# Stick-breaking attention in spans of 512 keys for both heads, with weights as a sigmoid times a running product

## The chip, the cores and the metric

One core of one Trainium2 chip runs the whole kernel. The metric is device time in microseconds of one launch, the median of three runs. TensorE (PE) multiplies, VectorE (DVE) and ScalarE (ACT) work elementwise and move results out of PSUM, GpSimd (POOL) builds masks and gathers rows, SyncE (SP) issues most transfers. The engines run their own instruction streams in order and meet only at semaphores.

## The reference, cut to what matters

One layer: a projection, three groups of heads side by side (RWKV-7, RG-LRU, stick-breaking attention), an output projection with LayerNorm, then a grouped top-2 MoE with LayerNorm. The change concerns the attention and a little of the MoE. SEQ is 1024, there are 6 attention heads of 64, and queries come in blocks of 128.

```python
def stick_breaking_attention(p, norm_g):
    ...
    for i in range(seq // SBA_BLOCK):
        q0 = i * SBA_BLOCK
        kv_len = q0 + SBA_BLOCK
        z = jnp.einsum('bhtd,bhsd->bhts', q[:, :, q0:kv_len], k[:, :, :kv_len]) * scale
        ...
        mask = s_idx < t_idx
        log_keep = jnp.where(mask, jax.nn.log_sigmoid(-z), 0.0)
        after = lax.cumsum(log_keep, axis=3, reverse=True) - log_keep
        attn = jnp.where(mask, jnp.exp(jax.nn.log_sigmoid(z) + after), 0.0)
        outs.append(jnp.einsum('bhts,bhsd->bhtd', attn, v[:, :, :kv_len]))
    ...
    return head_rms_norm(o, norm_g, SBA_HEADS)
```

So a weight is sigmoid(z) times the product of sigmoid(-z) over all later keys that the mask lets through.

## The kernel before

**Stages.** 0 to 373 us: projection, RG-LRU and the elementwise part of RWKV-7. 373 to 900: the RWKV-7 state recurrence in 12 batches, with the attention woven into it. 900 to 1036: output projection, LayerNorm, router logits. 1036 to 1080: routing. 1080 to 1560: MoE, 21 rounds of two experts. 1560 to 1604: last LayerNorm.

**Batches.** The recurrence is worked off by `mats_pe`, `mats_act` and `mats_dve`, for 3 pairs of heads times 4 batches. A batch starts with products and transposes (L646, L656, L660), masks them on DVE (L765), then inverts a triangular matrix in five levels: PE multiplies (L602, 8 small products), ACT copies the result (L742), PE multiplies twice (L602), DVE keeps parts of the two results (L762, one copy for T under `lower`, one for U under `upper`), and the next level starts once T is there. Then come L683 to L707, and four state steps (L719, L726 on PE, L797 on DVE) with `keep_clock` products on PE in between (L629). Below, a level window is the time from one U copy to the next, the tail is from the last U copy to the next batch, the seam is the start of a batch up to its first U copy.

**Attention units.** `side_by_side` runs such a generator and calls `sba_pe`, `sba_act` or `sba_dve` at each of its 16 gaps, always the next step j. A unit is one head and one query tile with all its keys (128 to 1024), 48 units, 4 steps each. Tiles come in the order 0, 7, 1, 6, 2, 5, 3, 4. Step kinds for unit u: kind 0, PE writes z (L917) and the mask (L919) to PS0, ACT takes |z|, exp and ln (L965, L967, L969); kind 1, DVE takes max(z, 0) (L997); kind 2, DVE scans (L977) and subtracts (L979); next unit's kind 0, ACT takes exp (L951). The weights are then transposed on PE (L932) in kinds 1 and 2, copied by DVE (L989), and multiplied with v (L940) in kind 3; ACT copies the output out (L955). The scan of the unit in a batch's last gap is put off to the batch's end.

**Norms.** After every fourth batch `rnorm_*` normalizes the RWKV heads of the pair and `snorm_*` those of finished attention pairs: sums on PE (L336), Ln and Exp on ACT (L857, L859; L1014, L1016), products on DVE (L872, L874, L877; L1026), with four attention steps in between. The next batch, or the output projection (L1123), waits for them.

**MoE round.** Products of gate and up (L1499), transposes of the next round's rows (`xg_transposes`, L1493), transposes of the hidden rows (L1529, L1534) after DVE's products (L1585), copies (L1589 on DVE, L1564 on ACT), product of down (L1499).

## Time and profile before

| what | us |
| --- | --- |
| three runs | 1601.74, 1605.48, 1607.90 |
| median | 1605.48 |
| profiled execution | 1605.52 |
| its span, first to last instruction | 1603.8 |
| projection and elementwise parts | 373 |
| batches with attention, and the norms among them | 527 |
| output projection, norm, logits | 136 |
| routing | 44 |
| MoE | 480 |
| last norm | 44 |

The profiled execution took 1605.52 us, of which 1603.8 lie between its first and last instruction. PE is busy for 89% of the span, DVE 37%, ACT 27%, POOL 6%; PE's granted clock was 0.944 of full on average. In rows of a timeline the first number is the start, the second the length, both us; the bracket tells how long the engine had been idle and what released it. In rows of groups, "busy, mean ns of one" stands behind the count.

### The profile page before, as it was taken

The page shows a single profiled execution, that of the slowest core. Times are in us where ns is not written, and L with a number is a line of the kernel's source. Part 1 is how long each engine was busy: PE and PEld are TensorE (multiplying, and loading weights), DVE is VectorE, ACT ScalarE, POOL GpSimd, SP SyncE. Part 2 cuts the span into 40 slices and gives each one's busy share as a digit, 9 for nine tenths or more (in the row PEclk, how much of TensorE's full clock was granted, in tenths as well). Part 3 has the DMA queues.
Part 4 walks back from the last instruction along what each step waited for, and adds up shares of the span by engine and source line. Part 5 has one row for each costly group of instructions (what it writes and reads, how often), then busy time and mean ns, then how long its engine had stood idle before and what let it go on. Part 6 is the DMA issues. An engine that isn't in the chain of part 4 may idle for free.

```text
span 1603.8 us, 22792 instructions
## 1 busy us (share of the span) xinstructions
PE 1422.8 (89%) x9346; PEld 763.4 (48%) x9346; DVE 597.4 (37%) x1010; ACT 431.4 (27%) x671; POOL 102.7 (6%) x177
## 2 busy tenths in 40 slices
PE   8999999998888788887888999839999999999980
PEld 3444444455666566655666455514444444444430
DVE  2143103444667566656666333361011101111017
ACT  1044123322444334443434311121111111111113
POOL 0000000001000000000000000000110111111110
PEclk9999999999999988997999999859999999999995
DMA  4110111000000000002000225068749949959415
GB/s 185 38 40 31 35 39 40 27 0 1 1 2 2 1 1 2 1 2 106 1 2 2 81 92 210 27 238 299 271 137 352 338 128 320 340 168 317 117 32 217
DMA packets 61012, 170.14 MB, mean 106 GB/s; under 512 B 3184, under 2 KB 3328, under 8 KB 60928
## 3 DMA queue, kind: packets, MB, share of 16 engines
q1 hardware_dynamic: 54384, 145.31, 24.4%
q0 software_dynamic: 6544, 23.62, 6.1%
q8 instruction: 63, 1.03, 0.3%
q14 instruction: 21, 0.17, 0.0%
HBM read 144.28 MB, written 24.64 MB: 105 GB/s over the span
## 4 chain that ended last, share of the span: by engine, by line
PE 74%; DVE 15%; ACT 4%; issue 4%; DMA 2%; SPq 0%; DVEq 0%; POOL 0%; POOLq 0%; ACTq 0%
PE PS L1499 27%; PE PS L193 16%; PE PS L1123 7%; PE PS L602 4%; PE PS L917 3%; DVE TT L977 3%; PE PS L202 3%; DVE XS L762 2%; PE PS L940 2%; DVE XS L765 2%; PE PS L1493 1%; PE PS L932 1%; PE PS L336 1%; DMA YT<-x1d,RK 1%; PE PS L683 1%
## 5 line engine op out<-in xcount | busy, mean ns | idle before, releaser
L1499 PE MATMUL PS<-RK,YT 128*64 128x512 f32 x736 | 323.6, 596 | 0.8 <-DVE YT L1589 0.8
L193 PE MATMUL PS<-XS 128*128 128x512 f32 x672 | 294.6, 598 | 7.1 <-DMA XS<-in_xT 6.9
L1499 PE MATMUL PS<-XS,YT 128*64 128x512 f32 x656 | 287.3, 595 | 6.4 <-DVE YT L1589 5.5
L193 PEld LDWEIGHTS PS<-XS 128*128 128x128 f32 x672 | 127.3, 191 | 172.6 <-issue 164.2
L1499 PEld LDWEIGHTS PS<-XS,YT 128*64 128x64 f32 x656 | 89.0, 138 | 171.8 <-issue 170.7
L602 PE MATMUL PS<-XS 64*64 64x64 f32 x2688 | 110.9, 231 | 36.3 <-DVE XS L762 24.7
L602 PEld LDWEIGHTS PS<-XS 64*64 64x64 f32 x2688 | 95.1, 143 | 54.6 <-DVE XS L762 39.1
L1585 DVE TENSOR_TENSOR YT<-YT,PS 128x256 f32<-128x256 f32 x42 | 15.8, 419 | 271.8 <-PE PS L1499 271.8
L1123 PE MATMUL PS<-RK,YT 128*128 128x512 f32 x256 | 111.1, 593 | 1.1 <-DVE YT L1026 1.1
L1499 PEld LDWEIGHTS PS<-RK,YT 128*64 128x64 f32 x736 | 99.8, 137 | 20.7 <-issue 20.7
L1499 PE MATMUL PS<-SQ,YT 128*64 128x512 f32 x424 | 104.0, 593 | 1.9 <-DVE YT L1589 1.9
L1123 PEld LDWEIGHTS PS<-RK,YT 128*128 128x128 f32 x256 | 48.1, 190 | 59.8 <-issue 57.9
L762 DVE COPY_PREDICATED XS<-lower,PS 128x512 f32<-128x512 uint8 x60 | 43.5, 726 | 80.6 <-PE PS L602 69.7
L1598 DVE TENSOR_SCALAR YT<-PS,RK 128x512 f32<-128x512 f32 x21 | 15.8, 751 | 142.6 <-PE PS L1499 142.6
L977 DVE TENSOR_TENSOR_SCAN TT<-XS,TT 128x128 f32<-128x128 f32 (+7 forms) x48 | 66.0, 1374 | 1.0 <-ACT XS L969 0.5
L917 PE MATMUL PS<-SQ 64*128 64x512 f32 (+3 forms) x144 | 65.1, 562 | 0.6 <-ACT TT L1014 0.6
L742 ACT COPY XS<-PS 128x512 f32<-128x512 f32 x60 | 35.1, 584 | 109.2 <-PE PS L602 108.3
L1499 PEld LDWEIGHTS PS<-SQ,YT 128*64 128x64 f32 x424 | 38.0, 137 | 49.7 <-issue 49.7
L940 PE MATMUL PS<-XS,SQ 128*64 128x128 f32 x432 | 59.8, 285 | 0.0
L762 DVE COPY_PREDICATED XS<-upper,PS 128x512 f32<-128x512 uint8 x60 | 43.2, 720 | 36.0 <-PE PS L602 35.4
L1488 POOL DMA_INDIRECT sums<-YT,RK x21 | 33.6, 1600 | 328.9 <-DVE YT L1598 328.9
L1499 PE MATMUL PS<-YT 128*64 128x512 f32 x120 | 53.6, 593 | 0.0
(361 smaller groups left out, 1760.7 us busy)
## 6 DMA issues: line engine op xcount, KB each, us to landing
XS<-in_w_in SPq DMA_DIRECT2D x21, 512.0 KB, 3.2
XS<-in_w_gate SPq DMA_DIRECT2D x5, 2048.0 KB, 12.3
XS<-in_w_upx SPq DMA_DIRECT2D x5, 2048.0 KB, 18.0
XS<-in_w_down SPq DMA_DIRECT2D x5, 2048.0 KB, 9.1
RK<-in_w_gate SPq DMA_DIRECT2D x5, 2048.0 KB, 20.2
RK<-in_w_upx SPq DMA_DIRECT2D x5, 2048.0 KB, 22.6
RK<-in_w_down SPq DMA_DIRECT2D x5, 2048.0 KB, 13.1
SQ<-in_w_gate SPq DMA_DIRECT2D x4, 2048.0 KB, 21.3
```

Source lines behind the costliest of these rows:

```text
L193: m = e.matmul(acc[:, half * HB:(half + 1) * HB], XS[:, 8 + n % 4, kt * P:(kt + 1) * P], XS[:, kt, half * HB:(half + 1) * HB], start=kt == ...
L202: m = e.matmul(acc[:, 0:SBA_W], XS[:, kt, i * P:(i + 1) * P], wv[:, kt, :], start=kt == 0, stop=kt == KT - 1)
L602: ins = e.matmul(acc[r, m * P + d * C:m * P + (d + 1) * C], left[r, m, r], right[r, m, r], start=True, stop=True)
L742: e.copy(M1[:, :, :], four(RB(3))).then_inc(s_ma, 1)
L762: return e.copy_predicated(x[:, :, :], mask[:, lv:lv + 1, :].broadcast_to([P, 4, P]), src)
L765: e.tensor_tensor(AM[:, m, :, :], four(RB(m)), mask4[:, :, :], ALU.mult).then_inc(s_md, 1)
L917: ins = e.matmul(PS[0][:, lo:hi], SQ[h, g, i * P:(i + 1) * P], SQ[h, 3 + g, lo:hi], start=True, stop=not last)
L940: ins = e.matmul(PS[1][h, HB + (i % 4) * P:HB + (i % 4 + 1) * P], SV[:, st, g * P + hh * HD:g * P + (hh + 1) * HD], ATb[u % 2][:, st * P:( ...
L977: e.tensor_tensor_scan(R_[:, ::-1], E_[:, ::-1], R_[:, ::-1], 0.0, ALU.add, ALU.add).then_inc(s_bd, 1)
L1123: ins = e.matmul(PS[i % 2][:, half * HB:(half + 1) * HB], YT[:, kt, i * P:(i + 1) * P], WO[kt][:, half * HB:(half + 1) * HB], start=kt == ...
L1488: e.indirect_dma_start(sums, bass.IndirectOffsetOnAxis(put_tok, 0), Yb, None, compute_op=ALU.add)\
L1499: ins = e.matmul(acc[r, :], rows[:, r], third_cols(n, k, at, HB), start=start, stop=stop)
```

## The change

**Attention.** A unit is now both heads of a pair, one query tile, and at most 512 keys. Tiles 4 to 7 have two units, the later keys first; 36 units. PE writes z of head 0 and head 1 to the two halves of PS0 in turn. ACT takes sigmoid(-z) and sigmoid(z) for both heads at once. DVE writes 1 (or the carried product) into the last column, scans each head with a running product from the later keys on, keeps the carry, and multiplies once for both heads. Weights are transposed head by head, copied by DVE head by head, and multiplied with v for both heads in turn, in two parts. A unit has 5 steps, a batch uses 15 gaps. A new z waits only for the sigmoids of the unit ahead, no longer for DVE.

Units per pair, in order, as keys per head (tile): 128 (0), 512, 512 (7), 256 (1), 384, 512 (6), 384 (2), 256, 512 (5), 512 (3), 128, 512 (4).

**MoE.** The transposes of the next rows are cut in two halves, the second behind the transposes of the hidden rows, and 16 instead of 10 `keep_clock` products stand ahead of the first round.

```diff
-        GAPS = 16
+        GAPS, KINDS = 15, 5
         def batch_step(b):
-            return GAPS * b + 4 * (b // NQ) - 1
+            return GAPS * b + 4 * (b // NQ)
...
+        SPANS = []
+        for n in range(NPAIR * NT):
+            i = n % NT // 2 if n % 2 == 0 else NT - 1 - n % NT // 2
+            kv = (i + 1) * P
+            cuts = [(HB, kv), (0, HB)] if kv > HB else [(0, kv)]
+            SPANS += [(n, n // NT, i, lo, hi, lo == cuts[0][0], lo == 0) for lo, hi in cuts]
...
-                wait(e, s_bd, BD * u)
+                wait(e, s_ba, BA * u)
+                wait(e, s_na, z_after_norm[0])
...
+                for hh, h in heads:
+                    ins = e.matmul(Z[:, hh, 0:w], SQ[h, g, i * P:(i + 1) * P], SQ[h, 3 + g, lo:hi],
+                                   start=True, stop=not first)
...
-                    e.activation(E_, E_, ACT.Exp).then_inc(s_ba, 1)
...
-                e.activation(E_, PS[0][:, 0:kv], ACT.Abs).then_inc(s_ba, 1)
-                e.wait_ge(s_ba, BA * u + 1)
-                e.activation(E_, E_, ACT.Exp, scale=-1.0).then_inc(s_ba, 1)
-                e.wait_ge(s_ba, BA * u + 2)
-                e.activation(E_, E_, ACT.Ln, bias=1.0).then_inc(s_ba, 1)
+                e.activation(E2[u % 2][:, :, 0:w], Z[:, :, 0:w], ACT.Sigmoid, scale=-1.0).then_inc(s_ba, 1)
+                wait(e, s_bv, u - 1)
+                e.activation(AT2[u % 2][:, :, 0:w], Z[:, :, 0:w], ACT.Sigmoid).then_inc(s_ba, 1)
...
-            e.tensor_tensor_scan(R_[:, ::-1], E_[:, ::-1], R_[:, ::-1], 0.0, ALU.add, ALU.add).then_inc(s_bd, 1)
+            for hh in range(2):
+                e.tensor_tensor_scan(R[:, hh, 0:w - 1][:, ::-1], keep[:, hh, 1:w][:, ::-1], keep[:, hh, 1:w][:, ::-1],
+                                     1.0 if first else carry[:, hh:hh + 1], ALU.mult, ALU.min).then_inc(s_bd, 1)
             wait(e, s_bd, BD * u + 2)
-            e.tensor_tensor(E_, PS[0][:, 0:kv], R_, ALU.subtract).then_inc(s_bd, 1)
+            if not last:
+                e.tensor_tensor(two(carry[:, :]), R[:, :, 0:1], keep[:, :, 0:1], ALU.mult).then_inc(s_bc, 1)
+                wait(e, s_bc, carried[u + 1])
+            wait(e, s_ba, BA * u + 2)
+            e.tensor_tensor(keep, AT2[u % 2][:, :, 0:w], R, ALU.mult).then_inc(s_bd, 1)
...
-                e.tensor_scalar_max(Rl[:, 0:kv], PS[0][:, 0:kv], 0.0).then_inc(s_bd, 1)
...
-            keep_clock(e, PS[0][:, 0:HB], 10)
+            keep_clock(e, PS[0][:, 0:HB], 16)
...
-                xg_transposes(e)
+                xg_transposes(e, 0)
...
+                xg_transposes(e, 1)
...
+                late = [j for j in range(batch_step(b) + GAPS - 3, batch_step(b) + GAPS) if j % KINDS == 2]
+                side_by_side(mats_dve, lambda e, j: sba_dve(e, j, j not in late), e, b)
```

The new program also differs in what the compiler puts between: loads of ACT's function tables. The first place is ACT in the norms behind the last pair (names: TT holds squares and factors, PS0, PS1 and PS3 the sums). Before:

```order
L850 ACTIVATE TT<-RK 128x1024 [waits rwkv_norm_dve]
L1014 ACTIVATE TT<-PS0,consts 128x1024 [waits head_norm_pe]
L1016 ACTIVATE TT<-TT 128x1024 [waits head_norm_act]
L1014 ACTIVATE TT<-PS1,consts 128x1024 [waits head_norm_pe]
L1016 ACTIVATE TT<-TT 128x1024 [waits head_norm_act]
L857 ACTIVATE TT<-PS3,consts 128x1024 [waits rwkv_norm_act,rwkv_norm_pe]
```

Now:

```order
L852 ACTIVATE TT<-RK 128x1024 [waits rwkv_norm_dve]
L1018 ACT_TABLE_LOAD
L1018 ACTIVATE TT<-PS0,consts 128x1024 [waits head_norm_pe]
L1020 ACT_TABLE_LOAD
L1020 ACTIVATE TT<-TT 128x1024 [waits head_norm_act]
L1018 ACT_TABLE_LOAD
L1018 ACTIVATE TT<-PS1,consts 128x1024 [waits head_norm_pe]
L1020 ACT_TABLE_LOAD
L1020 ACTIVATE TT<-TT 128x1024 [waits head_norm_act]
L859 ACT_TABLE_LOAD [waits rwkv_norm_act]
L859 ACTIVATE TT<-PS3,consts 128x1024 [waits rwkv_norm_pe]
```

Each Ln and each Exp has a load of its own ahead of it, here and in the eight tiles of the LayerNorm behind the output projection; before, one load (L234) ahead of the batches served for all. There are 32 loads more, counted in the two programs' lists.

The second place is DVE between two levels of the second batch of the second pair (lower: the T copy, upper: the U copy; PS1: transposed weights; PS0: z; TT: the running sum or product). Before, between levels 3 and 4, one head of 896 keys:

```order
L762 COPY_PREDICATED XS<-upper,PS2 128x512 [waits delta_pe,inverse_transposed_level]
L989 COPY XS<-PS1 128x128 [waits attn_v_in_psum,attn_transposed]
L997 TENSOR_SCALAR TT<-PS0 128x896 [waits attn_act,attn_dve,z_in_psum]
L989 COPY XS<-PS1 128x128 [waits attn_v_in_psum,attn_transposed]
L977 SCALAR_TENSOR_TENSOR TT<-XS,TT 128x896 [waits attn_dve,attn_act]
L979 TENSOR_TENSOR XS<-PS0,TT 128x896 [waits attn_dve]
L762 COPY_PREDICATED XS<-lower,PS3 128x512 [waits delta_pe,inverse_level]
```

Now, in the same batch between levels 4 and 5, two heads of 512 keys:

```order
L764 COPY_PREDICATED XS<-upper,PS2 128x512 [waits delta_pe,inverse_transposed_level]
L999 COPY XS<-PS1 128x384 [waits attn_v_in_psum,attn_transposed]
L980 COPY TT<-carry 128x2 [waits attn_carry_kept,attn_dve]
L983 SCALAR_TENSOR_TENSOR TT<-XS,carry 128x511 [waits attn_act]
L983 SCALAR_TENSOR_TENSOR TT<-XS,carry 128x511
L990 TENSOR_TENSOR XS<-XS,TT 128x1024 [waits attn_act,attn_dve]
L764 COPY_PREDICATED XS<-upper,PS2 128x512 [waits delta_pe,inverse_transposed_level]
```

The max is gone, one scan has become two, and a block of scans and product stands at other gaps: with 5 steps to a unit it falls on odd and even gaps in turn, where before it always fell on the gap ahead of an even level's copies.

The third place is PE at the end of the up product in the loop of a MoE round (YT: gathered or hidden rows). Before:

```order
L1493 MATMUL PS1<-ident,YT 128x128 x7
L1529 MATMUL PS2<-ident,YT 128x128 [waits hiddenT_copied,hidden_done]
L1534 MATMUL PS2<-ident,YT 128x128 [waits hiddenT_copied_2_act,hidden_done_2]
L1499 MATMUL PS3<-XS,YT 64x512 [waits y_dve,hiddenT_copied,y_act,weight_thirds_loaded2]
```

Now:

```order
L1498 MATMUL PS1<-ident,YT 128x128 x3
L1536 MATMUL PS2<-ident,YT 128x128 [waits hiddenT_copied,hidden_done]
L1541 MATMUL PS2<-ident,YT 128x128 [waits hiddenT_copied_2_act,hidden_done_2]
L1498 MATMUL PS1<-ident,YT 128x128 x4
L1505 MATMUL PS3<-XS,YT 64x512 [waits y_dve,hiddenT_copied,y_act,weight_thirds_loaded2]
```

Four of the eight row transposes have moved from ahead of the hidden transposes to behind them.

## Rows read from the trace of the kernel before

**Rows 1.** Stretches: length, busy PE, PEld, DVE, ACT, POOL, clock, DMA share, GB/s.
```profile
373.00:408.20 35.20, 29.23 (x431) 21.16 (x430) 21.17 (x38) 15.65 (x31) 4.64 (x8) 0.95 0.01 2
...
408.20:449.20 41.00, 34.78 (x480) 26.27 (x476) 26.48 (x47) 16.31 (x32) 4.08 (x4) 0.96 0.01 2
...
725.20:771.80 46.60, 40.88 (x471) 29.94 (x471) 26.49 (x43) 17.16 (x32) 2.35 (x4) 0.78 0.24 91
...
sum 527.40, PE 445.41 PEld 323.49 DVE 328.26 ACT 214.32 POOL 31.31; mean PE 29.69 PEld 21.57 DVE 21.88 ACT 14.29 POOL 2.09
```
**Rows 2.** Timeline of PE, first batch, levels with almost no attention.
```profile
381.25 0.68 PE L602 MATMUL PS<-XS 64*64 64x64 f32 x16 [0.42 <-DVE XS L762]
...
384.27 0.68 PE L602 MATMUL PS<-XS 64*64 64x64 f32 x16 [0.42 <-DVE XS L762]
```
**Rows 3.** Timeline of DVE, first batch of the second pair, levels 3 and 4.
```profile
559.49 0.73 DVE L762 COPY_PREDICATED XS<-lower,PS 128x512 f32<-128x512 uint8 x1 [2.93 <-PE PS L602]
...
560.93 1.21 DVE L997 TENSOR_SCALAR TT<-PS 128x1024 f32<-128x1024 f32 x1
562.25 2.29 DVE L977 TENSOR_TENSOR_SCAN TT<-XS,TT 128x1024 f32<-128x1024 f32 x1
564.57 1.23 DVE L979 TENSOR_TENSOR XS<-PS,TT 128x1024 f32<-128x1024 f32 x1
565.71 0.71 DVE L762 COPY_PREDICATED XS<-lower,PS 128x512 f32<-128x512 uint8 x1
```
**Rows 4.** Groups by shape, 373 to 900 us.
```profile
L940 PE MATMUL PS<-XS,SQ 128*64 128x128 f32 x432 | 59.8, 285 | 0.0
...
L917 PE MATMUL PS<-SQ 64*128 64x512 f32 x72 | 43.4, 700 | 0.0
...
L989 DVE COPY XS<-PS 128x512 f32<-128x512 f32 x18 | 12.4, 689 | 6.4 <-PE PS L932 6.4
...
L977 DVE TENSOR_TENSOR_SCAN TT<-XS,TT 128x512 f32<-128x512 f32 x6 | 7.4, 1234 | 0.0
```
**Rows 5.** Timeline of PE, first products of a batch; z of one head, 896 columns.
```profile
372.97 2.10 PE L646 MATMUL PS<-RK 64*128 64x256 f32 x16
...
443.55 1.77 PE L917 MATMUL PS<-SQ 64*128 64x512 f32 x4
```
**Rows 6.** Timeline of DVE at a seam, first pair.
```profile
449.65 2.02 DVE L977 TENSOR_TENSOR_SCAN TT<-XS,TT 128x896 f32<-128x896 f32 x1
```
**Rows 7.** Timeline of ACT, a table load in the projection.
```profile
98.66 1.28 ACT L234 ACT_TABLE_LOAD   x1
99.95 1.15 ACT L320 ACTIVATE RK<-RK,vec 128x1024 f32<-128x1024 f32 x1
```
**Rows 8.** Timeline of ACT, norms behind the last pair.
```profile
895.84 1.06 ACT L1016 ACTIVATE TT<-TT 128x1024 f32<-128x1024 f32 x1
```
**Rows 9.** Timeline of PE and DVE, end of a MoE round's up product.
```profile
1277.12 1.09 PE L1493 MATMUL PS<-ident,YT 128*128 128x128 f32 x8
1277.23 0.76 DVE L1585 TENSOR_TENSOR YT<-YT,PS 128x256 f32<-128x256 f32 x2 [12.81 <-PE PS L1499]
...
1278.05 0.38 PE L1529 MATMUL PS<-ident,YT 128*128 128x128 f32 x2
...
1278.47 0.42 DVE L1589 COPY YT<-PS 128x256 f32<-128x256 f32 x1 [0.49 <-PE PS L1529]
...
1279.04 0.61 PE L1499 MATMUL PS<-XS,YT 128*64 128x512 f32 x1 [0.39 <-DVE YT L1589]
```
**Rows 10.** Timeline of PE ahead of the first MoE round.
```profile
1072.56 4.26 PE L629 MATMUL PS<-restart,identb 128*128 128x512 bf16 x10
...
1077.99 1.09 PE L1493 MATMUL PS<-ident,YT 128*128 128x128 f32 x8 [1.17 <-DMA YT<-x1d,RK]
```
**Rows 11.** A stretch of two microseconds, columns as in rows 1.
```profile
567.00:569.00 2.00, 2.00 (x14) 1.24 (x11) 0.03 (x1) 1.35 (x2) 0.00 (x0) 0.50 0.01 4
```
**Rows 12.** The page's costliest groups, all of the run's U copies behind level products.
```profile
L762 DVE COPY_PREDICATED XS<-upper,PS 128x512 f32<-128x512 uint8 x60 | 43.2, 720 | 36.0 <-PE PS L602 35.4
```

More of the change, by code:

```diff
@@ L907, in sba_pe @@
                     return
-                g, i, hh, h, kv, ng = unit(u)
+                n, g, i, lo, hi, first, last = SPANS[u]
                 wait(e, s_pe, LRU_T + SBA_T + NT)
-                wait(e, s_bd, BD * u)
-                for pair in range(1, NPAIR - 1):
-                    if j == norm_step(pair) + 1:
-                        wait(e, s_na, 2 * (pair - 1) + 1)
-                for lo in range(0, kv, HB):
-                    hi = min(kv, lo + HB)
-                    last = hi == kv
-                    ins = e.matmul(PS[0][:, lo:hi], SQ[h, g, i * P:(i + 1) * P], SQ[h, 3 + g, lo:hi],
-                                   start=True, stop=not last)
-                ins = e.matmul(PS[0][:, kv - P:kv], identb[:, :], causal_neg[:, :], start=False, stop=True)
+                wait(e, s_ba, BA * u)
+                wait(e, s_na, z_after_norm[0])
+                z_issued[0] = u + 1
+                w = hi - lo
+                for hh, h in heads:
+                    ins = e.matmul(Z[:, hh, 0:w], SQ[h, g, i * P:(i + 1) * P], SQ[h, 3 + g, lo:hi],
+                                   start=True, stop=not first)
+                if first:
+                    for hh, h in heads:
+                        ins = e.matmul(Z[:, hh, w - P:w], identb[:, :], causal_neg[:, :], start=False, stop=True)
                 ins.then_inc(s_bz, 1)
@@ L924, in sba_pe @@
                 return
-            g, i, hh, h, kv, ng = unit(u)
-            if kind <= ng:
-                k = kind - 1
-                wait(e, s_ba, BA * u + 4)
-                wait(e, s_bt, groups(u) + k)
-                lo, hi = group(i, k)
-                for st in range(lo, hi):
-                    ins = e.transpose(PS[1][:, (st - lo) * P:(st - lo + 1) * P], Eb[u % 2][:, st * P:(st + 1) * P],
-                                      ident[:, :])
+            n, g, i, lo, hi, first, last = SPANS[u]
@@ L934, in sba_pe @@
+            tiles = range(lo // P, hi // P)
+            if kind <= 2:
+                hh = kind - 1
+                wait(e, s_bd, BD * (u + 1))
+                wait(e, s_bt, 2 * u + hh)
+                for k in range(len(tiles)):
+                    ins = e.transpose(PS[1][:, k * P:(k + 1) * P], E2[u % 2][:, hh, k * P:(k + 1) * P], ident[:, :])
                 ins.then_inc(s_bx, 1)
+                return
+            cut = (len(tiles) + 1) // 2
             if kind == 3:
-                wait(e, s_bt, groups(u + 1))
@@ L937, in sba_pe @@
-                if hh == 0:
-                    wait(e, s_bo, u // 2)
-                for st in range(i + 1):
+                wait(e, s_bt, 2 * u + 2)
+                if first:
+                    wait(e, s_bo, n)
+            ins = None
+            for k in (range(cut) if kind == 3 else range(cut, len(tiles))):
+                for hh, h in heads:
                     ins = e.matmul(PS[1][h, HB + (i % 4) * P:HB + (i % 4 + 1) * P],
-                                   SV[:, st, g * P + hh * HD:g * P + (hh + 1) * HD],
-                                   ATb[u % 2][:, st * P:(st + 1) * P], start=st == 0, stop=st == i)
+                                   SV[:, tiles[k], g * P + hh * HD:g * P + (hh + 1) * HD],
+                                   AT2[u % 2][:, hh, k * P:(k + 1) * P], start=first and k == 0,
+                                   stop=last and k == len(tiles) - 1)
@@ L958, in sba_act @@
                     return
[L959 to L960 removed]
+                w = SPANS[u][4] - SPANS[u][3]
                 wait(e, s_bz, u + 1)
@@ L1503, in moe_pe @@
             ahead(e, s_xgp, s_htp, s_htp2, s_y1)
-            keep_clock(e, PS[0][:, 0:HB], 10)
+            keep_clock(e, PS[0][:, 0:HB], 16)
             e.wait_ge(s_xg, 16)
-            xg_transposes(e)
+            for half in range(2):
+                xg_transposes(e, half)
             e.wait_ge(s_tab, 1)
```

89 lines of the change are left out of this document (42 added, 47 removed).

## The prediction

> **What bounds the kernel now.** I read the stretches first, then the timeline of each engine inside a batch, then the groups by shape. The change sits almost wholly in the 527.4 us of batches and norms; PE is busy 445 of them, DVE 328, ACT 214 [rows 1]. PE's share looks like the bound, but in a batch the engines take turns. A level with next to no attention takes 3.03 us from one first product to the next (381.25 to 384.27), PE, ACT, PE and DVE one after another [rows 2]. Where a block of attention stands on DVE between two levels, the T copy waits for it: with a head of 1024 keys max, scan and subtraction take 1.21, 2.29 and 1.23 us, and 6.22 us pass from T copy to T copy (559.49 to 565.71) [rows 3]. Over all windows I find a length of 3.03 us or of DVE's attention work plus 1.35 us, whichever is more; 4.7 + 1.35 is close to the 6.2 shown. Only where z or v products stand alone does PE set a window. So a batch is a chain that passes through three engines, and takes 35.2 us with little attention and 41.0 with a full share [rows 1].
>
> **PE's attention work.** z takes 43.4 us for the 512-column pieces alone, v products 59.8 [rows 4]. Products on two halves of the rows overlap when they alternate: the 16 instructions of L646 are 8 products of 256 columns, 2048 in all, and take 2.10 us; at the rate of a z, 896 columns in 1.77, they would take 4.0 [rows 5]. With both heads in turn z and v are halved; with the narrower z pieces this is some 64 us of PE's busy time. Transposes stay.
>
> **DVE's work.** The max goes, 1.21 us for 1024 columns. The scan keeps its price for a column: two of 512 are 2 x 1.234 = 2.47 against 2.29 [rows 3, 4]. The product should cost what the subtraction does, 1.23 (the other end, should PSUM have been its limit, is half of that; nearest row taken). A block for 2 x 512 columns is then 2.47 + 1.23 + 0.1 to 0.2 for the ends = 3.8 to 3.9 us, against 4.73 for one head of 1024. Copies keep their shapes mostly, 0.69 for 512 [rows 4]. Summed over 36 units against 48: about 149 against 181 us, 32 less.
>
> **What of it lies on the chain.** I went through the 12 batches gap by gap with these prices; the 60 windows between the U copies [rows 12] now add up to 260 us, the 12 tails to 141 (the norms left out), the 12 seams to 86.
> - Windows. Before, a block falls on the windows ahead of level 2's and level 4's copies, a third into the tail, a fourth is put off. Now two of a batch's three blocks fall into windows and the third is put off, so windows hold more of DVE than before, 55 us above their cover of 1.65 (3.03 less the two copies) against 40. Against it, PE and ACT hold windows up less: 22 us by my count, against 41 now in which slow-clock stretches are included. Of the 22, some 13 are new: when z falls on an even gap, the two sigmoids (2 x 1.06 us [rows 8], 1024 columns) stand ahead of ACT's next level copy and that window grows by some 2 us, z's own time included. Sum of the windows: 255, so -5.
> - Tails. No block stands there any more, and z and v are short: about 10.3 us each against 11.8, -18.
> - Seams. The put-off block runs ahead of the masks, as a scan of 2.02 us and its subtraction do now [rows 6]. In the first pair it is as long as now. In the later pairs it is 1.4 to 3.8 us, where now it is mostly 128 to 384 columns: +8. The first big unit of the third pair now falls behind the norms' last product, ahead of the next masks: +3. Sum +11.
> Together -12 us. It can be anything from -50 (PE sets every window, 64 us and a bit of ACT's relief come through) to +15 (second rival).
>
> **Norms.** Sigmoid, Ln and Exp now each need a table load. One takes 1.28 us, and the next instruction starts 0.01 us behind its end [rows 7]. There are 32 more, 41 us of ACT. Most hide: ACT waits for DVE or PE between norm tiles, and a load that has no wait of its own runs while the engine would be idle. Those on the path: behind the first pair the Exp (1.3, and 1.4 for the block now put off to that place); behind the second pair five loads less the wait for sums that covers one and a half of them, and larger sigmoids, +5; behind the last pair four in the row Ln, Exp, Ln, Exp that the output projection waits for [rows 8], +5.1; at the last LayerNorm tile one, +1.3. Sum +14, between +8 (loads hide behind sums) and +18.
>
> The Trainium skill, "ScalarE: Activation LUTs", section "What ACT_TABLE_LOAD costs", gives 2.66 us for a switch, 1.28 of load and 1.38 of drain. The row shows the first and nothing of the second. With the page's figure the ten or so loads on the path would cost, by estimate, 14 us more.
>
> **MoE.** Between the up product and the down product lie 1.92 us (1277.12 to 1279.04) for eight, two and two transposes, products on DVE and a copy. The hidden transposes start at 1278.05 though the first DVE half is there about 1277.65 (0.42 of the 0.76); the copy starts 0.42 us behind their start and ends at 1278.89, and PE follows 0.15 later [rows 9]. With four row transposes less ahead they start at about 1277.75, the copy ends at 1278.6, PE could go on at 1278.75, and its remaining transposes end there too. 0.29 x 21 rounds = -6 us; bounds 0 and -9. The next gather is issued behind POOL's scatter anyway, far later than the half of a transposition block by which it is now released later. Six more keep_clock products at 0.43 us [rows 10] reach 1079.4 where the rows arrive at 1077.99, against a first product that starts fast: 0, within 1.5 either way.
>
> **Sum.** 1605.5 - 12 + 14 - 6 = 1601.5, against the profiled execution, 1605.52; the median is 1605.48. I take **1601 us**.
>
> **Rivals.**
> - PE is what counts. Its share is highest, and its waits inside a full batch add up to only 6 of 41 us. If DVE's blocks merely fill time that PE's long z and v products (43.4 and 59.8 [rows 4]) would take anyway, two thirds of the 64 us come through: -40 + 14 - 6 = 1574. Against it: the window of rows 3, in which PE waits for DVE.
> - The slow clock. Behind DVE blocks of 3.9 us and more PE stood idle for 2 us or so, and was granted 0.50, that is 1.2 instead of 2.4 GHz, for several us after (567 to 569 [rows 11], right behind the block of rows 3); such a batch took 46.6 us at a clock of 0.78 [rows 1]. With PE's work halved and 23 big blocks in windows and seams against 14, more stretches run slow: nine more at 1 to 2 us, and the same cost as now for the others, which my windows left out, is +22: 1605.5 + 10 + 14 - 6 = 1624. It decides if most full batches run at clocks like that 0.78 and not like the 0.95 and 0.96 of the first two. This is the case on the other side.
> - A table switch costs the load twice, since the engine also has to run empty: ten loads on the path at another 1.28 make +13, 1614. Rows 7 speak against it, the following instruction starting at once; but there both neighbours were long ones. The skill's page named above has such a drain.
> - The change doesn't do what it says: z of two heads doesn't overlap. Then PE's saving is only v's, and the sum moves by a few us, inside the range.
>
> **Chances.** The sum's case 0.40, with its own range 1590 to 1613: 0.10 of it faster, 0.28 the same, 0.02 slower. PE's case 0.33, all faster. The slow clock 0.22, table switches 0.05, both slower. A measurement here can tell about 0.5% from no change, 8 us. So faster 0.43, same 0.28, slower 0.29. The range takes in most of both outer cases: 1564 to 1627.
>
> **What would show it.** Right: T copies wait up to 6 us behind blocks of two scans; three blocks in a batch; tails of about 10 us; ACT loads of 1.28 us, four in the last norms, where the output projection starts some 15 us after the last batch instead of 10; MoE rounds of 22.4 instead of 22.67 us. PE's case: full batches of 37 us. The slow clock: granted clock under 0.85 in full batches, and these over 42 us. Wrong altogether: a product on DVE far cheaper than the subtraction, scans dearer by the column, or z of two heads taking 1.7 us for 2 x 512 columns.

## The result, and the profile after

The changed kernel takes 1625.33 us (median of 4 runs, 1624.39 to 1626.59) against 1605.99 for the kernel before: ratio 1.0131, 95% interval 1.0109 to 1.0153. It is slower by 19 us, where 1601 was forecast. With each later group of runs the kernel before was run again and took 1604.92 to 1606.07 us (medians), so times of different groups can be set side by side to about 1 us. The profiled execution has a span of 1622.7 us against 1603.8, so the two traces show the same 19 us.

I cut both traces along the same instructions: a batch's seam (first product to the first U copy), its windows (U copy to U copy), its tail (last U copy to the next batch), and the norms.

| part, us | before | after | difference | forecast |
|---|---|---|---|---|
| 12 seams | 85.1 | 94.8 | +9.7 | +11 |
| 60 windows | 260.5 | 263.2 | +2.7 | -5 |
| 12 tails | 141.4 | 134.3 | -7.1 | -18 |
| norms between pairs | 30.4 | 40.1 | +9.7 | +7.7 |
| last norms, to the output projection | 10.0 | 15.4 | +5.4 | +5.1 |
| output projection and LayerNorm | 136.5 | 141.0 | +4.5 | +1.3 |
| MoE rounds | 471.1 | 465.3 | -5.8 | -6 |
| sum | | | +19.1 | -4 |

The page of the changed kernel, its first line and the row of PE (in the kernel before PE is busy 1422.8 us):

```profile
span 1622.7 us, 22622 instructions
...
PE 1394.9 (86%) x9352; PEld 708.1 (44%) x9352; DVE 569.8 (35%) x1004; ACT 405.4 (25%) x583; POOL 99.7 (6%) x177
```

PE has 28 us less to do, DVE 28 and ACT 26 less, and still the end comes later. Stretches of the changed kernel (columns as in rows 1), two full batches and the whole attention stage:

```profile
409.60:451.25 41.65, 34.64 (x473) 24.93 (x471) 23.42 (x45) 10.72 (x22) 2.35 (x4) 0.84 0.01 2
...
594.80:638.00 43.20, 34.55 (x475) 24.55 (x471) 23.59 (x45) 11.10 (x22) 2.35 (x4) 0.84 0.01 1
...
372.94:920.71 547.77, 413.70 (x5690) 295.80 (x5689) 298.71 (x543) 163.36 (x297) 28.18 (x48) 0.88 0.03 9
```

The second batch had a clock of 0.96 before and took 41.0 us [rows 1]; now it has 0.84 and takes 41.7. Over the stage the mean granted clock fell from 0.92 to 0.88. Where does PE wait? Groups by shape over 372 to 905 us, first of the kernel before (level products, then the products behind the last level):

```profile
L602 PE MATMUL PS<-XS 64*64 64x64 f32 x2688 | 110.9, 231 | 36.3 <-DVE XS L762 24.7 <-ACT XS L742 10.6
...
L683 PE MATMUL PS<-XS 64*64 64x128 f32 x192 | 17.6, 339 | 3.3 <-DVE XS L762 3.2
```

and of the changed kernel, with z (L916), v (L944) and the U copies:

```profile
L604 PE MATMUL PS<-XS 64*64 64x64 f32 x2688 | 116.4, 238 | 52.1 <-DVE XS L764 29.4 <-ACT XS L744 22.0
...
L764 DVE COPY_PREDICATED XS<-upper,PS 128x512 f32<-128x512 uint8 x60 | 43.0, 717 | 9.5 <-PE PS L604 8.5
...
L944 PE MATMUL PS<-XS,SQ 128*64 128x128 f32 x432 | 40.3, 300 | 3.4 <-DVE XS L999 3.2
...
L916 PE MATMUL PS<-SQ 64*128 64x512 f32 x72 | 27.3, 844 | 2.7 <-ACT TT L1018 2.7
...
L685 PE MATMUL PS<-XS 64*64 64x128 f32 x192 | 19.2, 361 | 18.5 <-DVE XS L764 18.5
```

z and v did shrink (43.4 and 59.8 us in rows 4, now 27.3 and 40.3). In their place PE waits: for DVE 47.9 us at these two lines against 27.9, for ACT 22.0 against 10.6. DVE waits 9.5 us ahead of the U copies, where it waited 36.0 [rows 12]: DVE is now seldom early. And the level products, the same work, take 116.4 us instead of 110.9; with PE's waits filled (experiment 1) they take 106.3 in the changed kernel, so this is the low clock.

One window shows all of it: the changed kernel, sixth batch, PE and DVE.

```profile
606.10 1.15 PE L604 MATMUL PS<-XS 64*64 64x64 f32 x32
606.44 0.95 DVE L983 TENSOR_TENSOR_SCAN TT<-XS 128x383 f32<-128x383 f32 x1
...
607.31 0.93 DVE L983 TENSOR_TENSOR_SCAN TT<-XS 128x383 f32<-128x383 f32 x1
...
608.47 0.96 DVE L990 TENSOR_TENSOR XS<-XS,TT 128x768 f32<-128x768 f32 x1
609.34 0.72 DVE L764 COPY_PREDICATED XS<-lower,PS 128x512 f32<-128x512 uint8 x1
609.95 0.71 DVE L764 COPY_PREDICATED XS<-upper,PS 128x512 f32<-128x512 uint8 x1
...
610.12 0.69 PE L604 MATMUL PS<-XS 64*64 64x64 f32 x16 [2.50 <-DVE XS L764]
...
611.57 1.97 PE L604 MATMUL PS<-XS 64*64 64x64 f32 x32
```

Two scans, carry and product hold the T copy up until 609.34; PE stands for 2.50 us, and soon after its next 32 products take 1.97 us instead of the 1.15 of the first line. The clock of the same place:

```profile
610.00:611.00 1.00, 0.89 (x19) 0.81 (x20) 0.66 (x2) 0.16 (x1) 0.00 (x0) 0.83 0.00 0
611.00:612.00 1.00, 0.85 (x12) 0.48 (x12) 0.00 (x0) 0.70 (x2) 0.00 (x0) 0.50 0.00 0
...
616.00:617.00 1.00, 1.00 (x14) 0.88 (x11) 0.00 (x0) 1.00 (x2) 0.00 (x0) 0.50 0.00 0
```

0.50 is 1.2 instead of 2.4 GHz. By the shares of these rows it begins about 0.5 us after PE took up work at 610.12, and it lasts 6.8 us, through a z and half of the next window.

### The profile page after: what moved, and what is told of

Same layout as the page of the kernel before. It is cut to its first block, busy times and chain, and to the rows that moved or that the text cites. A ratio compares the mean times of both kernels' runs of the same rounds, so it can differ in the third digit from the quotient of the medians.

```text
span 1622.7 us, 22622 instructions
## 1 busy us (share of the span) xinstructions
PE 1394.9 (86%) x9352; PEld 708.1 (44%) x9352; DVE 569.8 (35%) x1004; ACT 405.4 (25%) x583; POOL 99.7 (6%) x177
## 4 chain that ended last, share of the span: by engine, by line
PE 72%; DVE 13%; ACT 6%; issue 5%; DMA 2%; SPq 0%; DVEq 0%; POOL 0%; POOLq 0%; ACTq 0%
PE PS L1505 26%; PE PS L195 16%; PE PS L1128 7%; PE PS L604 4%; DVE TT L983 3%; PE PS L204 3%; PE PS L916 2%; DVE XS L764 2%; DVE XS L767 2%; PE PS L1498 1%; PE PS L933 1%; PE PS L631 1%; DMA YT<-x1d,RK 1%; PE PS L338 1%; PE PS L685 1%
## 5 line engine op out<-in xcount | busy, mean ns | idle before, releaser
L604 PE MATMUL PS<-XS 64*64 64x64 f32 x2688 | 116.4, 238 | 52.1 <-DVE XS L764 29.4
L604 PEld LDWEIGHTS PS<-XS 64*64 64x64 f32 x2688 | 100.5, 150 | 80.0 <-DVE XS L764 42.3
L999 DVE COPY XS<-PS 128x512 f32<-128x512 f32 (+3 forms) x72 | 39.8, 552 | 59.9 <-PE PS L933 59.9
L1505 PEld LDWEIGHTS PS<-SQ,YT 128*64 128x64 f32 x424 | 32.6, 137 | 52.8 <-issue 52.8
L1493 POOL DMA_INDIRECT sums<-YT,RK x21 | 33.6, 1601 | 321.3 <-DVE YT L1606 321.3
L1578 ACT ACTIVATE YT<-PS,RK 128x512 f32<-128x512 f32 x21 | 14.4, 687 | 138.2 <-PE PS L1505 138.2
L226 DVE SCALAR_TENSOR_TENSOR RK<-PS,vec,RK 128x1023 f32<-128x1023 f32 x11 | 14.1, 1283 | 97.6 <-ACT RK L215 97.6
L617 POOL TENSOR_TENSOR XS<-RK,pc 128x256 f32<-128x256 f32 x24 | 14.2, 613 | 548.2 <-PE PS L204 368.2
```

The source lines that it names most:

```text
L604: ins = e.matmul(acc[r, m * P + d * C:m * P + (d + 1) * C], left[r, m, r], right[r, m, r], start=True, stop=True)
L999: e.tensor_copy(AT2[v % 2][:, hh, 0:w], PS[1][:, 0:w]).then_inc(s_bt, 1)
L1493: e.indirect_dma_start(sums, bass.IndirectOffsetOnAxis(put_tok, 0), Yb, None, compute_op=ALU.add)\
L1505: ins = e.matmul(acc[r, :], rows[:, r], third_cols(n, k, at, HB), start=start, stop=stop)
```

## The experiments

Theory: DVE's block of attention is one piece of 3.9 us where a window covers 1.65; PE's narrower work turns into waiting for it, and the longer waits bring the low clock. On top, the table loads cost more than forecast. Rivals: the blocks hold the windows but the clock hits only hidden work; PE's busy time counts for nothing, or for everything; the price of the table loads is not their own length.

**1. Filling PE's waits, in the changed kernel and in the kernel before.** `fill_before` is true where a scan stands in the window, FILL is 6.

```
+                if fill_before(b, lv):
+                    keep_clock(e, RB(3), FILL)
                 wait(e, s_tl, b * NTL + lv)
                 diag_products(e, RB(3), AM[:, :, 1, :], T_, ms)
```

> The changed kernel with six 512-column products that nobody reads put on PE ahead of each level product whose T copy has a DVE block of attention in front of it (some 20 places; at full clock six take 1.3 us, and PE stands idle for 2 to 2.7 us there). Slow-clock theory (the rival with 1624 of the prediction: behind such a wait PE is granted 0.50 for several us, and the stage's mean clock fell from 0.92 to 0.88): the clock of the attention stage rises to 0.93 or more and the time falls by 8 to 18 us, to 1607 to 1617. Rival, the DVE blocks alone hold the windows and the low clock hits only products that are hidden: the clock rises, the time stays within 3 us of 1625. Should the filling itself come late in some windows, up to +5.

1613.33 us, ratio to the kernel before 1.0058 (1.0038 to 1.0077), 12 us less than the changed kernel. The stage's clock up to 850 us is 0.92 instead of 0.88, windows 254.0 us, tails 132.1, seams and norms as they were. The place shown above, with the filling:

```profile
602.61 1.47 PE L631 MATMUL PS<-restart,identb 128*128 128x512 bf16 x6
...
605.18 0.68 PE L604 MATMUL PS<-XS 64*64 64x64 f32 x16 [1.10 <-DVE XS L772]
...
606.63 1.15 PE L604 MATMUL PS<-XS 64*64 64x64 f32 x32 [0.41 <-ACT XS L752]
```

DVE's block is as long as before, only the products behind it are fast again. So these low stretches were on the path. The same in the kernel before, with its own scans:

> The kernel before with the same filling: six 512-column products on PE, read by nobody, ahead of each level product whose window has a DVE scan in it. The prediction took the cost of the slow clock to be the same before and after and left it out of both; the filling took 12 us off the changed kernel. If the low clock is a cost that the change brought: here within 4 us of 1605 (0 gain), or slower, since PE has 22 to 28 us more of z and v work to delay. If both kernels lose alike by it: 8 to 12 us faster, and the low clock doesn't explain the difference between them.

1602.36 us, ratio 0.9983 (0.9968 to 0.9998): 3 us, with the clock at 0.97 instead of 0.91. That is 9 us less than in the changed kernel, but it doesn't follow that those 9 are a cost of the change, for the filling also delays PE where it has work. Two batches of the kernel before with filling, the second and the ninth:

```profile
411.81:454.61 42.80, 37.19 (x491) 27.17 (x488) 26.45 (x46) 16.41 (x32) 4.08 (x4) 0.96 0.01 2
728.82:770.86 42.04, 37.68 (x484) 27.04 (x484) 26.23 (x44) 17.04 (x32) 2.36 (x4) 0.94 0.27 101
```

Without it [rows 1] they took 41.0 us at a clock of 0.96 and 46.6 at 0.78: the first has lost by the filling, the second gained. Window by window, the 14 windows of the kernel before whose clock had been under 0.95 became 12 us shorter and the other 46 became 12 us longer; in the changed kernel 24 such windows became 13 us shorter and the other 36 4 us longer. So low clock in the windows costs both kernels about the same, 12 and 13 us, and most of the 9 us are what the filling itself costs. Each total is a lower bound of what the low clock costs, and the difference of two lower bounds is no bound of anything.

More of the changed kernel does run slow: at half clock are 60 us of its windows against 46 before, 22 of its seams against 14, and 27 of the nine tails with no norm behind against 16. Work at half the clock loses at most half of its length, so these 34 us more can by estimate cost up to 17. How much they do cost no run here shows: the filling doesn't stand in seams and tails.

**2. The DVE block taken apart.** Both scans and the carry stay in `sba_scan`, the product is now `sba_product` and follows two gaps later:

```
             if kind == 2 and scan:
                 sba_scan(e, u)
+            if kind == 4 and scan:
+                sba_product(e, u)
```

> The changed kernel with each DVE block taken apart: both scans and the carry stay where the block was, the product follows two gaps later. Theory that DVE's block holds the chain: a window has some 1.65 us of DVE cover, a block of 2 x 512 columns is 3.9 us, so it costs about 2.2 us of a window; in two pieces of 2.6 and 1.25 us it costs about 1.0. With some 20 such blocks in windows the time falls by 15 to 25 us, to 1600 to 1610, and PE's waits of 2.5 us shrink to 1.3, with fewer stretches at 0.50. Rival, PE and ACT hold the windows (sigmoids on even gaps, v products): within 4 us of 1625, or slower, since transposes of the unit now wait for the later product.

1577.89 us, ratio 0.9826 (0.9797 to 0.9855): 47 us less than the changed kernel, twice what was expected. In the profiled execution, which took 1581.88 us, windows are 233.1 (-30), seams 87.7 (-7), tails 127.5 (-7). 33 of the 60 windows had a clock of 0.95 or more in both traces; they are 13.5 us shorter in all, up to 1.3 us each where a block stood. The other 27, slow in one trace or in both, gave 16.6. The same window as above:

```profile
595.21 0.72 DVE L764 COPY_PREDICATED XS<-lower,PS 128x512 f32<-128x512 uint8 x1
...
595.99 0.68 PE L604 MATMUL PS<-XS 64*64 64x64 f32 x16 [1.52 <-DVE XS L764]
596.44 0.95 DVE L996 TENSOR_TENSOR XS<-XS,TT 128x768 f32<-128x768 f32 x1
...
597.45 1.15 PE L604 MATMUL PS<-XS 64*64 64x64 f32 x32 [0.41 <-ACT XS L744]
```

The product now runs while PE works, PE waits 1.52 us and stays fast. Is the clock's share in the 47? Filling on top of it:

> The changed kernel with scans and product two gaps apart and the same filling. Taking the block apart brought 47 us where 15 to 25 were expected from the cover of a window alone. If the rest came through the clock (shorter waits of PE, fewer stretches at half clock), the 12 us of the filling are in it already: within 3 us of 1578, or slower. If the two are independent: 1566.

1581.29 us, ratio 0.9831 (0.9806 to 0.9855): no gain. The 12 us of the filling and the 47 of the split are not independent. Between the two kernels with filling the split is still worth 32 us (1613.33 against 1581.29), and seams, windows and tails (norms left out) hold 39 instead of 61 us at half clock. Those 22 us can by estimate account for 11 at most, so at least some 20 of the 47 us are the chain itself.

**3. The same treatment for the kernel before**, its subtraction (`sba_minus`) one gap behind its scan:

```
             if kind == 2 and scan:
                 sba_scan(e, u)
+            if kind == 3 and j not in [norm_step(g) for g in range(NPAIR)]:
+                sba_minus(e, u)
```

> The kernel before with its own DVE block taken apart in the same way: the scan stays at its gap, the subtraction follows one gap later (at once in the one unit behind which the head norms run). This asks what the changed form of the weights is worth when both kernels have short pieces on DVE. Theory that the length of one piece of DVE work between two level copies is what costs: a head of 1024 keys leaves pieces of 1.21, 2.29 and 1.23 us, so the time falls by 10 to 25 us, to 1580 to 1595, and the form of the weights itself is worth little. Rival, splitting helps the changed form only, since here the z of the next unit must wait for the subtraction and the pieces of one unit stand in three windows anyway: 1598 to 1615.

1592.57 us, ratio 0.9902 (0.9868 to 0.9935): 13 us; seams 78.6 instead of 85.1, windows 256.5 instead of 260.5. Long pieces on DVE are a cost of both kernels; by these two edits, which are alike but not the same, it is three to four times dearer in the changed one. With both taken apart the changed kernel is 15 us ahead, of which 6 are MoE's.

**4. Table loads.** The three norms' loads by hand; `exp_ln` loads one set that has both functions, `sigmoid_set` that of Sigmoid:

```
+            if snorms(g):
+                exp_ln(e)
             for xg in snorms(g):
                 snorm_act(e, xg, 1)
+            if snorms(g):
+                sigmoid_set(e)
...
+            exp_ln(e)
             wait(e, s_fp, 3 * g + 3)
```

> The changed kernel with the table loads of the head norms placed by hand: one load of the set that holds both Ln and Exp ahead of each Ln-Exp group, before its wait, and one load of Sigmoid's set behind the group, in place of one load ahead of each Ln, Exp and first Sigmoid. LayerNorm tiles unchanged. If loads on the path cost their 1.28 us each (two behind the first pair, four or so behind the second, four behind the last): 8 to 12 us faster, 1613 to 1617. If they had been hidden beside PE's sums and DVE: within 3 us of 1625. If a load also makes the engine run empty (another 1.28 to 1.38 us): 16 to 20 us faster.

1614.51 us, ratio 1.0070 (1.0044 to 1.0096): 11 us less. Last norms in the changed kernel, ACT:

```profile
909.76 1.28 ACT L1018 ACT_TABLE_LOAD   x1
...
912.19 1.28 ACT L1020 ACT_TABLE_LOAD   x1
```

with two more at 914.56 and 916.99, and with the loads by hand:

```profile
907.06 1.28 ACT L239 ACT_TABLE_LOAD   x1
...
912.66 1.28 ACT L235 ACT_TABLE_LOAD   x1
...
913.95 1.28 ACT L239 ACT_TABLE_LOAD   x1
```

From the last batch to the output projection it is now 11.45 us instead of 15.4, norms between pairs 37.2 instead of 40.1. Projection and LayerNorm take 136.5 again as before, instead of 141.0. The expectation said that the LayerNorm's tiles stay as they are, and that was wrong: the set loaded by hand for the last norms has both functions, so all 16 loads of the eight tiles are gone, and 4.5 of the 11 us lie there. (The two loads side by side at 912.66 are my own waste: Sigmoid's set is not needed any more behind the last pair.) And without any load:

> The changed kernel with both sigmoids replaced by an exponential of next to nothing (a scale of 1e-33), so that Exp, Ln and the rest share one table set and no loads stand in the attention stage, the norms and the LayerNorm tiles. The attention weights are therefore not those of the reference, the rows may be routed to other experts, and only the time up to the router is read. If loads are all that the norms lost: norms between the pairs 30 to 33 us instead of 40.1, the last norms 10 to 11 instead of 15.4, last LayerNorm tile 2.5 us shorter; 15 to 20 us in all up to the router. If the sigmoid itself were the dear operation, its 1.02 us for 1024 columns would fall as well.

One run, of which only the time up to the router is read (it takes 1651.54 us in all, with 23 MoE rounds instead of 21): last norms 10.02 us, projection and LayerNorm 136.5, norms between pairs 32.5. Loads are all that the last norms and the projection lost; between the pairs they are 7.6 of the 9.7 us. The exponential takes the same 1.02 us for 1024 columns as the sigmoid. Four loads in the last norms cost 15.4 - 10.0 = 5.4 us, 1.35 each. So an ordinary load costs what its row shows. The Trainium skill, "ScalarE: Activation LUTs", section "What ACT_TABLE_LOAD costs", gives 2.66 us for a switch with its drain, by which these four would by estimate have made 10.6; the measurement decides against it here.

**5. Sigmoids behind the level copy.** The two sigmoids of a unit that falls on an even gap (k = 10, 6 and 2 in the first, second and third pair) run at the next one:

```
+                    if k % 2 == 0 and 0 < k < 11 and j % KINDS == 0:
+                        held.append(j)
+                    else:
+                        sba_act(e, j)
```

> The changed kernel with the two sigmoids of a unit that fall on an even gap of the inverse put off by one gap, behind ACT's copy of the level. The prediction put some 13 us of window time down to the sigmoids standing ahead of that copy (2 x 1.06 us for 1024 columns): then 5 to 12 us faster, 1613 to 1620, windows with z in an even gap shorter by about 1 to 2 us. Rival: these windows are set by z and its weight loads on PE, and DVE's scan then starts late instead: within 3 us of 1625, or slower.

1609.16 us, ratio 1.0019 (1.0003 to 1.0035): 16 us less. In the third pair the window with z falls from 4.8 to 3.6 us in all four batches. The changed kernel there:

```profile
756.36 1.02 ACT L966 ACTIVATE XS<-PS 128x1024 f32<-128x1024 f32 x1 [0.93 <-PE PS L916]
...
758.19 0.59 ACT L744 COPY XS<-PS 128x512 f32<-128x512 f32 x1
...
758.92 1.15 PE L604 MATMUL PS<-XS 64*64 64x64 f32 x32 [1.41 <-ACT XS L744]
```

PE waits for a copy that is queued behind two sigmoids. With these put off:

```profile
746.63 0.58 ACT L744 COPY XS<-PS 128x512 f32<-128x512 f32 x1 [3.01 <-PE PS L604]
...
747.36 1.15 PE L604 MATMUL PS<-XS 64*64 64x64 f32 x32 [0.19 <-ACT XS L744]
```

Windows are 7.6 us shorter, tails 5.0. Only 1.1 of the 5.0 lie in the first pair, where k = 10 stands in the tail; in the other pairs nothing was moved in the tails, and their 3.9 us are indirect, presumably clock. The remark on batches without such a gap in the expectation of the combined run below was wrong: every pair has one.

**6. What PE's time is worth.** Each z issued twice:

```
+                for hh, h in heads:
+                    e.matmul(Z[:, hh, 0:w], SQ[h, g, i * P:(i + 1) * P], SQ[h, 3 + g, lo:hi], start=True, stop=True)
                 for hh, h in heads:
```

> The changed kernel with each unit's z products issued twice into the same PSUM (the first result is overwritten), which adds to PE about the 44 us that z takes in the changed kernel, near the 64 us by which the change narrows PE's attention work. If PE's busy time were what counts (the rival with 1574): 25 to 40 us slower, 1650 to 1665. If DVE's blocks hold the windows and PE waits for them: z stands in a gap whose window has no block in most cases, so it should still cost a part, 10 to 20 us, 1635 to 1645. If PE's work is all but free: within 5 us of 1625.

1650.12 us, ratio 1.0276 (1.0249 to 1.0303): 25 us more. Its z products, the pieces of 512 columns of both copies:

```profile
L916 PE MATMUL PS<-SQ 64*128 64x512 f32 x72 | 27.2, 842 | 2.7 <-ACT TT L1020 2.7
L918 PE MATMUL PS<-SQ 64*128 64x512 f32 x72 | 22.3, 699 | 0.0
```

Over all shapes z grew by 34.5 us of PE, so 0.7 us of time for one of PE, at the lower edge of what the PE rival expected. The sigmoids also start later by the second copy, and the run doesn't tell the two apart. PE's work in gaps is not free. If a us taken away is worth as much as one added, which no run shows, narrowing z and v gained some tens of us by itself. That what the change put on DVE and ACT in one piece ate it is borne out by experiments 2, 5 and 7, in which this work is cut and moved and PE's attention work stays the same.

**7. Everything together.** The scan of one head, the scan of the other with the carry, and the product each one gap apart, with the loads by hand; then the sigmoids put off as well; then the filling. Two pieces and the loads came first. In the three pieces `sba_scan` is one head's scan and `one_scan` the other's, with the carry:

```
+            if kind == 2:
+                sba_scan(e, u)
+            elif kind == 3:
+                one_scan(e, u, 1)
+            else:
+                sba_product(e, u)
```

> Both edits that helped the changed kernel together: scans and product two gaps apart, and table loads placed by hand ahead of the Ln-Exp groups. They touch different stretches, so the gains should add: 47 and 11 us off 1625, 1567. If the loads had been hidden once the norms start at another point of the units: 1574 to 1578.

> Table loads by hand, and the DVE block in three pieces instead of two: scan of one head, scan of the other with the carry, product, each one gap apart. Pieces are then about 1.3 us, under the 1.65 us that a window covers, though two gaps share a window. Theory of the longest stretch of DVE work in a window: up to another 10 us below the 1568.8 of two pieces, 1558 to 1565, mostly at the seams of the later pairs, where one scan instead of two stands ahead of the masks. Rival, with two gaps to a window the same two scans still stand in one window half the time: within 4 us of 1569.

> The same, and the two sigmoids of a unit on an even gap put off behind ACT's copy of the level, which took 16 us off the changed kernel by itself (half of it in batches where no sigmoid stood on an even gap, so a part must be clock). With short pieces on DVE the windows in which ACT is late should be the longest left: 5 to 12 us below the run without it. If the sigmoids' delay now makes the first scan late: no gain or up to 5 us slower.

> The same, and six 512-column products on PE ahead of the level products that wait for a DVE scan, as in the run that took 12 us off the changed kernel. If short pieces have already removed the idle stretches behind which the clock falls: no gain, or 2 to 6 us slower, since PE's filling (1.3 us at full clock) is longer than what is left of the wait. If the clock is still granted at half behind many windows: 3 to 8 us faster.

| kernel | us | ratio to before | windows | tails | clock to 850 us |
|---|---|---|---|---|---|
| two pieces, loads | 1568.78 | 0.9775 (0.9738 to 0.9812) | 229.6 | 127.3 | 0.92 |
| three pieces, loads | 1550.07 | 0.9649 (0.9624 to 0.9674) | 217.6 | 124.0 | 0.94 |
| and sigmoids put off | 1535.30 | 0.9565 (0.9539 to 0.9591) | 205.9 | 119.1 | 0.96 |
| and filling | 1544.69 | 0.9618 (0.9593 to 0.9643) | 218.9 | 119.5 | 0.97 |

The third of these beats both kernels, by 70 and by 90 us. Only the first came out as expected: the third piece brought 19 us where 10 at most were expected, the sigmoids 15 where 12 were, and the filling, worth 12 us at first, now costs 9 where 6 at most were. The window of the sixth batch in the third kernel:

```profile
577.49 0.95 DVE L998 TENSOR_TENSOR_SCAN TT<-XS 128x383 f32<-128x383 f32 x1
...
578.36 0.70 DVE L767 COPY_PREDICATED XS<-lower,PS 128x512 f32<-128x512 uint8 x1
...
579.12 0.68 PE L607 MATMUL PS<-XS 64*64 64x64 f32 x16 [0.45 <-DVE XS L767]
579.56 0.94 DVE L998 TENSOR_TENSOR_SCAN TT<-XS 128x383 f32<-128x383 f32 x1
...
580.79 0.96 DVE L1011 TENSOR_TENSOR XS<-XS,TT 128x768 f32<-128x768 f32 x1
```

PE's wait of 2.50 us is down to 0.45. Over the stage (372 to 822 us), level products and the products behind the last level:

```profile
L607 PE MATMUL PS<-XS 64*64 64x64 f32 x2688 | 103.7, 222 | 23.2 <-ACT XS L747 13.2 <-DVE XS L767 8.8
...
L688 PE MATMUL PS<-XS 64*64 64x128 f32 x192 | 14.0, 288 | 8.4 <-DVE XS L767 8.2
```

17 us of waiting for DVE instead of 47.9, and the same products in 103.7 and 14.0 us instead of 116.4 and 19.2.

**8. MoE's part alone**, in the kernel before:

> The kernel before with only the MoE part of the change: row transposes in two halves around the hidden ones, and 16 in place of 10 of the keep_clock products. The profile of the changed kernel shows the MoE part 5.8 us shorter (rounds of 22.48 in place of 22.67 us, and the first round 1.6 us shorter): 1600 us. If that gain came only from the cores' clock history in that run, within 2 us of 1606.

1599.19 us, ratio 0.9957 (0.9938 to 0.9976), as expected. The end of an up product in the changed kernel: the hidden transposes (L1536) start 0.60 us after the row transposes, and the down product 1.73 us after the row transposes, where rows 9 show 1.92. The two edits of MoE were not run one by one.

```profile
1253.39 0.66 PE L1498 MATMUL PS<-ident,YT 128*128 128x128 f32 x4
...
1253.99 0.44 PE L1536 MATMUL PS<-ident,YT 128*128 128x128 f32 x2
...
1255.12 1.08 PE L1505 MATMUL PS<-SQ,YT 128*64 128x512 f32 x4
```

## Why the prediction was wrong

- **What bounds the kernel**: right in kind. A window is as long as its turns or as its DVE work, and splitting that work moved the time as nothing else did. But the prediction took the cover of 1.65 us as a fixed discount on a sum. The lever was how the same DVE work is cut: 47 us (part of them clock) lay in one product's place, and the text never priced a block as one piece against two.
- **PE's attention work**: z and v overlap as said. z of 2 x 512 columns takes 1.13 us at full clock (598.53 us in the trace of experiment 2); v was to be halved and was not: it fell from 59.8 to 40.3 us, and with hardly any low clock left (the third kernel of experiment 7) it still takes 38.2. The rival that PE's time is what counts had its price nearly right (two thirds then, 0.7 measured by adding work), and what it left out is what the change added elsewhere.
- **DVE's work**: right. Product 1.22, scan 1.21 to 1.27 for 511 columns, DVE 28 us less busy against 32 said.
- **Windows, -5 against +2.7**: the failing step, first half, is the term of the sum for PE and ACT in the windows, "22 us by my count, against 41 now in which slow-clock stretches are included". The low clock was in the number for before and not in the one for after. The changed kernel has 60 us of its windows at half clock, against 46; filling PE's waits in them took 13 us off the slow ones and left the sum at 254.0, against the 255 of the count.
- **Tails, -18 against -7.1**: the second half, 11 us. They were taken as free of blocks, which they are, and as running at full clock, which they don't: 8 of 12 run at half clock for over half of their first 2 us (6 before). In the second and third pair a block stands in the last window, and PE waits 18.5 us ahead of L685, the products behind the last U copy, against 3.2; that wait still counts in the window, the slow clock behind it falls into the tail. The filling did not stand there and left the tails at 132.1. Short pieces and late sigmoids together made the tails 119.1, below the 123 of the forecast.
- **Sigmoids on even gaps**, 13 us in the windows' sum: right in place. Putting them off brought 16 us, of which 7.6 lie in the windows.
- **Seams, +11 against +9.7**: right in the sum. 2.5 us of it lie in the first pair, where none was forecast, and 7 in the later ones, where 11 were.
- **Norms and LayerNorm, +14 against +19.6**: a size. The loads on the path were counted well up to the projection (+12.8 forecast, +15.1 measured). The step on the last LayerNorm tile was wrong. The prediction let a load that "has no wait of its own" run in idle time, and where that is so it does: behind the first pair the load starts at once and its activation waits. But the first load of the tile does have a wait, and starts only when its activation's input is there, after 10.81 us of idleness; the second stands in the row behind it:

```profile
539.99 1.28 ACT L859 ACT_TABLE_LOAD   x1
544.25 1.11 ACT L859 ACTIVATE TT<-PS,consts 128x1024 f32<-128x1024 f32 x1 [2.98 <-PE PS L338]
...
1049.64 1.28 ACT L1088 ACT_TABLE_LOAD   x1 [10.81 <-DVE RK L1075]
...
1051.25 1.28 ACT L1090 ACT_TABLE_LOAD   x1
```

  That is 2.6 us and not 1.3. Another 2.0 us came where nothing was priced. The output projection's first products, before and now:

```profile
900.36 27.73 PE L1123 MATMUL PS<-RK,YT 128*128 128x512 f32 x64 [1.12 <-DVE YT L1026]
...
920.71 29.69 PE L1128 MATMUL PS<-RK,YT 128*128 128x512 f32 x64 [6.53 <-DVE YT L1031]
```

  PE stands for 6.53 us ahead of them instead of 1.12, and begins them with a granted clock of 0.50 (from 921 to 923 us).
- **MoE, -6 against -5.8**: right in the sum, by luck. A round was to gain 0.29 us and gained 0.19, 4 us in 20 rounds; the rest comes from the first round, 1.6 us shorter, for which 0 was forecast.
- **The rivals**: the slow clock was the one that came about, at the very time it gave, 1624. That is partly luck. Its threshold ("most full batches at clocks like 0.78") was not reached: ten full batches have 0.83 to 0.92, five of them take over 42 us. It priced 22 us more for the batches, which came out 17 us over the forecast (+5.3 against -12), and how much of the 17 is clock no run tells; norms and table loads, 5.6 us over, made up the rest. A chance of 0.22 for a case whose mechanism the trace of before already showed (rows 11) was too low, and above all it should have been a term of the sum. The drain behind a table load is refuted by experiment 4.

What stays open: how the split's 47 us divide into clock and chain. At least some 20 are chain by the estimate in experiment 2; the rest can't be divided by these runs, since a shorter wait of PE changes both. Open too is what the low clock in seams and tails costs.

## What to carry to other kernels

Where three engines take turns, as here, price the work in the gaps by the longest piece between two turns, not by its sum alone. Cut it into pieces shorter than the cover, and check which gap each falls on, ahead of or behind the copy that the next engine waits for: here the cut, the place of the sigmoids and the loads together were worth 90 us on a form of the weights that lost 19 as first placed. Where the trace shows half clock behind PE's waits and a change makes these longer, count it in the sum and not as a side case, and on both sides of the comparison. Filling the waits helps only where they are long: the same filling took 12 us off one kernel here and cost another 9. When an activation from another table set enters, look at how many loads the compiler puts in, and load by hand one set for each group, one that holds all its functions.

## What the runs showed of the hardware

- Whether a table load placed by the compiler runs in idle time differs from place to place: ahead of L859, behind the first pair, it started at once and the activation then waited 2.98 us; ahead of L1088 it started after 10.81 us of idleness, when the activation's input was there, and its 1.28 us lay on the path.
- PE fell to half clock about 0.5 us after it took up work behind a wait of 2.50 us, and not in the same place of the program behind a wait of 1.52 us, nor behind one of 1.10 us with filling ahead of it. In the batches of the changed kernel 15 waits of PE of 2.2 to 3.2 us began at full clock, and the clock fell during or within 1.6 us behind all of them; of 24 waits of 1.0 to 2.2 us it did so at 5. That is a count of one trace, not a limit.
- The same 2688 level products take 116.4 us in the changed kernel and 103.7 in the third kernel of experiment 7, where none of them runs at half clock.
- Doubling z cost 0.7 us for each us of PE, in a stage where PE also waits 70 us for others at the level products and those behind them. So most of the added work did not fall into these waits.
